# HGRN2 recurrence of a two-layer transformer: pair products of two neighbouring levels in one TensorE visit

## The chip, the cores and the metric

The kernel runs on one NeuronCore of a Trainium2 chip. The core has five engines that run side by side and meet at semaphores: TensorE (PE) for matrix products, VectorE (DVE) and ScalarE (ACT) for elementwise work, GpSimd (POOL), here for one kind of subtraction only, and SyncE (SP), which issues the transfers. The metric is the device time of one execution in microseconds; lower is better.

## The reference

Three blocks follow one another on 512 tokens of width 1024: a block with three mixers and a gated feed-forward part, a layer with an HGRN2 recurrence and a convolved feed-forward part, and a layer with latent attention. The change touches only the recurrence:

```
def _chunk_gated_recurrence(q, k, v, log_f):
    # S_t = diag(exp(log_f_t)) S_{t-1} + k_t v_t^T ; o_t = S_t^T q_t, chunkwise
    ...
        G = jnp.cumsum(gc, axis=2)
        ...
        diff = G[:, :, :, None, :] - G[:, :, None, :, :]
        decay = jnp.where(causal, jnp.exp(jnp.where(causal, diff, 0.0)), 0.0)
        scores = jnp.einsum("bhtd,bhsd,bhtsd->bhts", qc, kc, decay)
        o_intra = jnp.einsum("bhts,bhse->bhte", scores, vc)
```

There are 8 heads of width 128. For each head q, f (the forget gate), v (the values) and g (the output gate) are projections of the normed input.

## The kernel before

**Weights.** The products with weights are done in three parts, high half times high half, low times high and high times low, so that each 128 x 128 block of weights costs three matmuls of 512 columns (`products`, lines 228 to 230 of the profile). A unit is 8 such blocks. It comes in by a transfer, ACT makes its high half (`high`, L203) and POOL its low half in two instructions (L2900, L2901), in four slots that are used in turn. One projection tile is one unit: 24 matmuls, of which `pe_tile` can do a quarter (6 matmuls) at a time.

**Levels.** The causal scores of a head are taken in blocks of 128 tokens. Inside a block they are split by distance into seven levels of width 64, 32, 16, 8, 4, 2 and 1 (`LEVELS`, numbered 0 to 6), with the diagonal by itself ("own"). Each level passes through four steps:

- DVE takes the distances of the cumulated logarithms, two subtractions of 256 elements (`dve_distances`, L2038 and L2039).
- ACT takes their exponent (`act_decays`, L1939).
- DVE multiplies by key and query, 512 elements (`dve_factors`, L2048).
- PE makes the pair products in small tiles (`pe_level`, `pe_pairs`, L1777, 32 small matmuls for levels 2 to 6), and DVE copies the wanted half of them by a mask into the tile `diag` (`dve_keep_level`: a one-element copy at L2064 that only waits, and the copy at L2060).

Even levels go to one PSUM bank and odd ones to another, and `pe_level` waits for the copy of the level two before. The levels' operands take turns in four places, so `dve_distances` waits for the pair products of four levels before.

**Order on PE.** `pe_head(i)` writes the order by hand. It starts with `pe_attend(i - 1)` (L1742, L1745), which multiplies `diag` of the previous head by its values and so waits for the last copied level, 6, of that head. Then follow own and level 0, the tile f of head i + 1, the transposes of v (L422) and level 1. After that come the sum of squares of the previous head (`pe_finish`, L298), the products between blocks (`pe_across`, L1806), and the tiles q, g and v, in parts between the levels. `pe_across` waits for the previous head's `head_rstd` on ACT. In head 0 there are fewer tiles to place, so it holds matmuls whose results nobody reads (`pe_keep_busy`, L410). Head 7 has no next head; in place of tiles it takes steps of the output projection (`pe_project_step`, 9 matmuls each).

**Order on DVE.** `dve_head(i)` is written by hand too. From own on it runs: copy of own (L2171), `to_end` (L2175), copy of level 0, low squares (L2155), distances 3, factors 2, `dve_across` (L2141 to L2146), f, then copy of level 1, distances 4, factors 3, `dve_forget` (L2071 to L2077), `dve_normed` of the head before (L2121), q, copy 2, distances 5, factors 4, `dve_cum` (a scan, L2085), `dve_gated` (L2129), copy 3, distances 6, factors 5, `dve_low_out` (L2134), copy 4, factors 6, g, distances 0 of the next head, copy 5, distances 1 of the next head, copy 6. f, q, g and v leave PSUM at L402.

**Order on ACT.** `act_head` is not changed. It takes the decays in the order 2, 3, 4, 5, 6 and then 0 and 1 of the next head, and makes the highs of weight units in between. One is made after decays 6 and the copy of the products between blocks (L2005).

Of the kernel before, what the change touches and what calls it, by code (L numbers as in the profile page):

```python
# [27 lines left out]
LEVELS = (64, 32, 16, 8, 4, 2, 1)  # L28
# [206 lines left out]
def pe_tile(m, t, event, out, xh, xl, quarters=range(4)):  # L235

    base = take_unit(m, t)
    w = TILE
    for q in quarters:
        pairs = [(kb, xh[:, kb * w:(kb + 1) * w], xl[:, kb * w:(kb + 1) * w]) for kb in (2 * q, 2 * q + 1)]  # L240
        ins = products(m, t, out, base, pairs, start=q == 0, stop=q == 3)
        if q == 3:
            ins.then_inc(*m.U.mark(*event))
            t.unit += 1
# [162 lines left out]
def pe_keep_busy(m, t, bank, widths):  # L407

    for w in widths:
        t.op.matmul(bank[:, 0:w], m.col("ones", 0, P), m.col("levels", 0, w), start=True, stop=True)  # L410
# [1307 lines left out]
def level_bank(n):  # L1718
    return 0 if n % 2 else 3
# [49 lines left out]
def pe_pairs(m, t, left, right, event, bank, w):  # L1769


    n = max(w, 32)
    for c in range(0, S, P):
        for o in range(0, P, n if w < 32 else 2 * n):
            rows = slice(c + o, c + o + n)
            cols = rows if w < 32 else slice(c + o + n, c + o + 2 * n)
            ins = t.op.matmul(m.ab(bank)[o:o + n, cols], left[:, rows], right[:, cols], start=c == 0, stop=c == S - P,  # L1777
                              skip_group_check=True)
    ins.then_inc(*m.T.mark(*event))


def pe_level(m, t, i, n):
    x = Head(m, i).xs[n]
    t.wait_ge(*m.V.at("hgrn", "factors", i, n))
    if n > 1:
        t.wait_ge(*m.V.at("hgrn", "kept", i, n - 2))
    elif n:
        t.wait_ge(*m.V.at("hgrn", "kept_own", i))
    elif not i:
        t.wait_ge(*m.A.at("hgrn", "rstd"))  # L1790
    pe_pairs(m, t, x, x, ("hgrn", "pairs", i, n), level_bank(n), LEVELS[n])
# [18 lines left out]
def pe_head(m, t, i):  # L1810
    x = Head(m, i)
    last = i == KD - 1

    def f_tile():
        if i:
            t.wait_ge(*m.V.at("hgrn", "f", i))
        pe_tile(m, t, ("hgrn", "f", i + 1), f_bank(m, i + 1), m.nh, m.nl)

    def q_tile(quarters):
        t.wait_ge(*(m.A.at("hgrn", "o", i - 1) if i else m.V.at("hgrn", "q", 0)))  # L1820
        pe_tile(m, t, ("hgrn", "q", i + 1), m.gb(1), m.nh, m.nl, quarters)

    def g_tile(quarters):
        if i:
            t.wait_ge(*m.V.at("hgrn", "g", i - 1))
        pe_tile(m, t, ("hgrn", "g", i), m.gb(3), m.nh, m.nl, quarters)

    def v_tile(quarters):
        t.wait_ge(*m.A.at("hgrn", "vtok", i))
        pe_tile(m, t, ("hgrn", "v", i + 1), m.gb(2), m.nh, m.nl, quarters)  # L1830

    if i:
        pe_attend(m, t, i - 1)
    else:
        g_tile(range(4))
        f_tile()
    t.wait_ge(*m.V.at("hgrn", "key", i))
    t.wait_ge(*m.A.at("hgrn", "q", i))
    pe_pairs(m, t, x.key, x.qs, ("hgrn", "own", i), 0, 0)
    pe_level(m, t, i, 0)  # L1840
    if i and not last:
        f_tile()
    t.wait_ge(*m.V.at("hgrn", "v", i))
    pe_to_tokens(m, t, ("hgrn", "vtok", i), m.gb(2), x.vt, TB)
    if last:
        g_tile((0, 1))
    pe_level(m, t, i, 1)
    if i:
        pe_finish(m, t, i - 1)
    if last:  # L1850
        g_tile((2, 3))
    else:
        q_tile((0, 1))
    pe_level(m, t, i, 2)
    if last:
        pe_project_step(m, t, 0)
    else:
        q_tile((2, 3))
    pe_across(m, t, i)
    if last:  # L1860
        pe_project_step(m, t, 1)
    elif i:
        g_tile((0, 1))
    else:
        v_tile((0,))
    pe_level(m, t, i, 3)
    if last:
        pe_project_step(m, t, 2)
    elif i:
        g_tile((2, 3))  # L1870
    else:
        v_tile((1,))
    for n in range(4, len(LEVELS)):
        pe_level(m, t, i, n)
        if last:
            if n < 6:
                pe_project_step(m, t, n - 1)
        elif i:
            v_tile((0, 1) if n == 4 else (n - 3,))
        elif n < 6:  # L1880
            v_tile((n - 2,))
        if i == 0 and n in (4, 6):
            pe_keep_busy(m, t, m.gb(0), (512, 512) if n == 4 else (512, 512, 512))


def pe_project_step(m, t, kb):

    t.wait_ge(*m.V.at("hgrn", "low_out", kb))
    if kb == 0:
        t.wait_ge(*m.A.at("hgrn", "o", KD - 2))  # L1890
        t.wait_ge(*m.A.at("hgrn", "vtok", KD - 1))
    pe_wide(m, t, kb, [("ffn1", "projected", j) for j in range(WIDE)], m.bigr[:, 0:8 * TILE], m.bigr[:, 8 * TILE:16 * TILE])
# [138 lines left out]
def dve_distances(m, v, i, n):  # L2031
    x, w = Head(m, i), LEVELS[n]
    (g0, g1), (x0, x1) = halves(x.cum, w), halves(x.xs[n], w)
    mid = g0[:, :, w - 1:w].broadcast_to([P, S // (2 * w), w])
    before = level_before(i, n, 4)
    if before:
        v.wait_ge(*m.T.at("hgrn", "pairs", *before))
    v.op.tensor_tensor(x0, mid, g0, ALU.subtract)  # L2038
    v.op.tensor_tensor(x1, g1, mid, ALU.subtract).then_inc(*m.V.mark("hgrn", "distances", i, n))  # L2039


def dve_factors(m, v, i, n):
    x, w = Head(m, i), LEVELS[n]
    v.wait_ge(*m.A.at("hgrn", "decays", i, n))
    if n == 0:
        v.wait_ge(*m.A.at("hgrn", "q", i))
    xs = segments(x.xs[n], w)
    v.op.tensor_tensor(xs, xs, left_and_right(x.pair, w), ALU.mult).then_inc(*m.V.mark("hgrn", "factors", i, n))  # L2048


def dve_keep_level(m, v, i, n):

    w, pairs = LEVELS[n], P // (2 * LEVELS[n])
    mask = halves(m.col("levels", n * P, P), w)[1].bitcast(U32)
    mask = mask.broadcast_to([P, TB, w]) if pairs == 1 else mask.unsqueeze(1).broadcast_to([P, TB, pairs, w])
    part = lambda ap: blocks(ap).rearrange("p c (n a w) -> p c n a w", a=2, w=w)[:, :, :, 1, :]
    v.wait_ge(*m.T.at("hgrn", "pairs", i, n))
    v.wait_ge(*(m.V.at("hgrn", "kept", i, n - 1) if n else m.V.at("hgrn", "kept_own", i)))
    dve_wait_only(m, v)
    v.op.copy_predicated(part(Head(m).diag), mask, part(m.ab(level_bank(n)))).then_inc(*m.V.mark("hgrn", "kept", i, n))  # L2060
# [97 lines left out]
def dve_head(m, v, i):  # L2158
    x = Head(m, i)
    last = i == KD - 1  # L2160

    dve_factors(m, v, i, 0)
    dve_factors(m, v, i, 1)
    dve_distances(m, v, i, 2)
    if i:
        dve_v(m, v, i)
    v.wait_ge(*m.T.at("hgrn", "own", i))
    v.wait_ge(*(m.T.at("hgrn", "out", i - 1) if i else m.V.at("hgrn", "cleared")))
    dve_wait_only(m, v)
    mask = m.col("ident", 0, P).bitcast(U32).unsqueeze(1).broadcast_to([P, TB, P])  # L2170
    v.op.copy_predicated(blocks(x.diag), mask, blocks(m.ab(0))).then_inc(*m.V.mark("hgrn", "kept_own", i))  # L2171
    if i:
        v.wait_ge(*m.T.at("hgrn", "cross", i - 1))
    end = blocks(x.cum)[:, :, P - 1:P].broadcast_to([P, TB, P])
    v.op.tensor_tensor(blocks(x.kb), end, blocks(x.cum), ALU.subtract).then_inc(*m.V.mark("hgrn", "to_end", i))  # L2175
    dve_keep_level(m, v, i, 0)
    if i:
        dve_head_square_low(m, v, i - 1)
    dve_distances(m, v, i, 3)
    dve_factors(m, v, i, 2)  # L2180
    dve_across(m, v, i)
    if not last:
        dve_f(m, v, i + 1)
    dve_keep_level(m, v, i, 1)
    dve_distances(m, v, i, 4)
    dve_factors(m, v, i, 3)
    if not last:
        dve_forget(m, v, i + 1)
    if i:
        dve_normed(m, v, i - 1)  # L2190
    if not last:
        dve_q(m, v, i + 1)
    dve_keep_level(m, v, i, 2)
    dve_distances(m, v, i, 5)
    dve_factors(m, v, i, 4)
    if not last:
        dve_cum(m, v, i + 1)
    if i:
        dve_gated(m, v, i - 1)
    dve_keep_level(m, v, i, 3)  # L2200
    dve_distances(m, v, i, 6)
    dve_factors(m, v, i, 5)
    if i:
        dve_low_out(m, v, i - 1)
    dve_keep_level(m, v, i, 4)
    dve_factors(m, v, i, 6)
    dve_g(m, v, i)
    if not last:
        dve_distances(m, v, i + 1, 0)
    dve_keep_level(m, v, i, 5)  # L2210
    if not last:
        dve_distances(m, v, i + 1, 1)
    dve_keep_level(m, v, i, 6)


# [908 lines left out]
```

## Time and profile before

| | before |
|---|---|
| median of 3 runs | 2015.29 us (2014.92 to 2015.47) |
| the profiled execution | 2015.5 us, span 2013.7 us |
| granted TensorE clock | 1.000 of full speed over the span |
| PE busy | 1993.1 us, 99% of the span |
| DVE, ACT, POOL busy | 48%, 47%, 43% of the span |
| recurrence, heads 0 to 7 | about 820 to 1060 us of the span |
| DVE busy in 877 to 908 us (one head) | 28.42 of 31 us |
| DVE busy in 820 to 846 us (head 0) | 25.38 of 26 us |

An engine's busy share is an average over the span. The chain that ended last is 92% PE. Times in the rows below are microseconds from the span's start. A row of the timeline holds the start, the duration, the engine, the line and what is written from what, and in brackets how long the engine idled before it and what released it. A vector instruction's listed duration overlaps the next one's start by some 0.08 us, so for a run of them the distance from start to start is what counts.

### The profile page before, as it was taken

The page shows a single profiled execution, that of the slowest core. Times are in us where ns is not written, and L with a number is a line of the kernel's source. Part 1 is how long each engine was busy: PE and PEld are TensorE (multiplying, and loading weights), DVE is VectorE, ACT ScalarE, POOL GpSimd, SP SyncE. Part 2 cuts the span into 40 slices and gives each one's busy share as a digit, 9 for nine tenths or more (in the row PEclk, how much of TensorE's full clock was granted, in tenths as well). Part 3 has the DMA queues.
Part 4 walks back from the last instruction along what each step waited for, and adds up shares of the span by engine and source line. Part 5 has one row for each costly group of instructions (what it writes and reads, how often), then busy time and mean ns, then how long its engine had stood idle before and what let it go on. Part 6 is the DMA issues. An engine that isn't in the chain of part 4 may idle for free.

```text
span 2013.7 us, 26586 instructions
## 1 busy us (share of the span) xinstructions
PE 1993.1 (99%) x10917; PEld 1621.0 (80%) x10917; DVE 975.9 (48%) x1511; ACT 940.9 (47%) x1322; POOL 860.7 (43%) x670
## 2 busy tenths in 40 slices
PE   9999999999999999999999999999999999999999
PEld 7788888878888887677777888888877788888887
DVE  6644443254201315898984553255157645522551
ACT  6666663353223225666664543244267645432441
POOL 2344334526544543443334544444431255444443
PEclk9999999999999999999999999999999999999999
DMA  6122222223232221121212223222210222322231
GB/s 259 53 94 74 74 74 94 95 74 105 95 104 94 94 99 58 64 74 64 75 64 94 94 98 102 88 101 97 86 48 27 79 94 95 101 98 92 97 102 66
DMA packets 51817, 178.31 MB, mean 89 GB/s; under 512 B 5744, under 2 KB 8944, under 8 KB 51568
## 3 DMA queue, kind: packets, MB, share of 16 engines
q1 hardware_dynamic: 51696, 176.61, 26.0%
q8 instruction: 87, 1.43, 0.3%
q14 instruction: 34, 0.28, 0.0%
HBM read 174.49 MB, written 2.10 MB: 88 GB/s over the span
## 4 chain that ended last, share of the span: by engine, by line
PE 92%; DVE 5%; ACT 2%; issue 1%; DMA 0%; POOL 0%; SPq 0%; ACTq 0%; DVEq 0%; POOLq 0%
PE ps_gemm L228 24%; PE ps_gemm L230 24%; PE ps_gemm L229 24%; PE ps_attend L228 4%; PE ps_attend L230 4%; PE ps_attend L229 4%; PE ps_attend L912 1%; PE ps_attend L1777 1%; PE ps_attend L2620 1%; PE ps_attend L2687 1%; PE ps_attend L2622 0%; PE ps_attend L925 0%; PE ps_attend L2621 0%; PE ps_attend L285 0%; ACT weights_high L203 0%
## 5 line engine op out<-in xcount | busy, mean ns | idle before, releaser
L2900 POOL TENSOR_TENSOR weights_low<-weights_raw,weights_high 128x512 fp32r<-128x512 f32 (+1 forms) x331 | 433.0, 1308 | 1108.0 <-ACT weights_high L203 1107.8
L228 PE MATMUL ps_gemm<-normed_high,weights_high 128*128 128x512 f32 x1665 | 658.3, 395 | 3.9 <-DVE normed_low L1322 3.3
L230 PE MATMUL ps_gemm<-normed_low,weights_high 128*128 128x512 f32 x1665 | 646.9, 389 | 0.0
L229 PE MATMUL ps_gemm<-normed_high,weights_low 128*128 128x512 f32 x1665 | 646.4, 388 | 0.0
L203 ACT ACTIVATE weights_high<-weights_raw 128x1024 fp32r<-128x1024 f32 (+1 forms) x340 | 339.4, 1006 | 447.0 <-PE ps_attend L230 215.6
L2901 POOL TENSOR_TENSOR weights_low<-weights_raw,weights_high 128x512 fp32r<-128x512 f32 (+1 forms) x331 | 437.8, 1323 | 0.0
L228 PEld LDWEIGHTS ps_gemm<-normed_high,weights_high 128*128 128x128 f32 x1665 | 312.6, 188 | 74.3 <-DVE normed_low L1322 5.0
L230 PEld LDWEIGHTS ps_gemm<-normed_low,weights_high 128*128 128x128 f32 x1665 | 312.6, 188 | 65.0
L229 PEld LDWEIGHTS ps_gemm<-normed_high,weights_low 128*128 128x128 f32 x1665 | 312.8, 188 | 63.5 <-issue 1.9
L228 PE MATMUL ps_gemm<-operands_high_low,weights_high 128*128 128x512 f32 (+1 forms) x552 | 216.1, 392 | 0.8 <-ACT weights_high L203 0.3
L230 PE MATMUL ps_gemm<-operands_high_low,weights_high 128*128 128x512 f32 (+1 forms) x552 | 214.1, 388 | 0.0
L229 PE MATMUL ps_gemm<-operands_high_low,weights_low 128*128 128x512 f32 (+1 forms) x552 | 214.0, 388 | 0.0
L402 DVE TENSOR_TENSOR scratch<-ps_gemm,rstd 128x512 f32<-128x512 f32 x89 | 60.7, 687 | 215.3 <-PE ps_gemm L230 198.6
L402 DVE TENSOR_TENSOR squares<-ps_gemm,rstd 128x512 f32<-128x512 f32 x106 | 73.1, 689 | 160.8 <-PE ps_gemm L230 130.0
L1491 ACT ACTIVATE ps_attend<-squares,parameters 128x512 f32<-128x512 f32 x88 | 68.9, 783 | 170.1 <-DVE squares L402 170.1
L228 PE MATMUL ps_attend<-operands_high_low,weights_high 128*128 128x512 f32 (+1 forms) x336 | 127.5, 379 | 2.6 <-DVE operands_high_low L321 1.6
L230 PE MATMUL ps_attend<-operands_high_low,weights_high 128*128 128x512 f32 (+1 forms) x336 | 126.5, 376 | 0.0
L229 PE MATMUL ps_attend<-operands_high_low,weights_low 128*128 128x512 f32 (+1 forms) x336 | 126.5, 376 | 0.0
L228 PEld LDWEIGHTS ps_gemm<-operands_high_low,weights_high 128*128 128x128 f32 x552 | 103.7, 188 | 23.2 <-issue 1.1
L230 PEld LDWEIGHTS ps_gemm<-operands_high_low,weights_high 128*128 128x128 f32 x552 | 103.6, 188 | 21.2
L229 PEld LDWEIGHTS ps_gemm<-operands_high_low,weights_low 128*128 128x128 f32 x552 | 103.7, 188 | 20.9 <-issue 0.2
L1551 DVE SCALAR_TENSOR_TENSOR ps_attend<-squares,parameters,ps_attend 128x511 f32<-128x511 f32 x88 | 66.4, 755 | 76.1 <-ACT ps_attend L1491 76.1
(340 smaller groups left out, 2179.1 us busy)
## 6 DMA issues: line engine op xcount, KB each, us to landing
weights_raw<-weights_full SPq DMA_DIRECT2D x317, 512.0 KB, 3.2
weights_raw<-weights_short SPq DMA_DIRECT2D x24, 128.0 KB, 2.0
residual<-x_tiles SPq DMA_DIRECT2D x4, 512.0 KB, 7.5
out_tiles<-residual SPq DMA_DIRECT2D x8, 256.0 KB, 2.1
parameters<-params SPq DMA_DIRECT2D x1, 1559.5 KB, 10.4
scratch<-memory_tiles SPq DMA_DIRECT2D x2, 256.0 KB, 4.9
scratch<-memory_tiles SPq DMA_DIRECT2D x1, 512.0 KB, 5.8
scratch<-positions SPq DMA_DIRECT2D x1, 256.0 KB, 10.6
```

The source lines that it names most:

```text
L203: s.op.activation(m.wh[:, j * UNIT:j * UNIT + w], m.raw[:, j * UNIT:j * UNIT + w], ACT.Copy).then_inc(m.s_hi, 1)
L228: t.op.matmul(out, m.wh[:, c:c + P], xh, start=start and n == 0, stop=False, skip_group_check=True)
L229: t.op.matmul(out, m.wl[:, c:c + P], xh, start=False, stop=False, skip_group_check=True)
L230: ins = t.op.matmul(out, m.wh[:, c:c + P], xl, start=False, stop=stop and n == len(pairs) - 1, skip_group_check=True)
L402: return v.op.tensor_tensor(dst, ps, m.rstd[:, 0:dst.shape[1]], ALU.mult)
L912: ins = t.op.matmul(zb[:, o:o + S - j * P], neg_tri if j == kb else neg_ones, x[:, ZOFF[j]:ZOFF[j] + S - j * P], start=False, stop=False, ...
L1491: s.op.activation(y, m.sq_tile(half), ACT.Identity, bias=m.col(f"conv_b{n - 1}", c), scale=m.col(f"conv_w{n - 1}", 88 + c)).then_inc(*m.A. ...
L1551: v.op.scalar_tensor_tensor(out=y[:, 1:S], in0=u[:, 0:S - 1], scalar=w(1), in1=y[:, 1:S], op0=ALU.mult, op1=ALU.add).then_inc(*m.V.mark(st ...
L1777: ins = t.op.matmul(m.ab(bank)[o:o + n, cols], left[:, rows], right[:, cols], start=c == 0, stop=c == S - P, skip_group_check=True)
L2620: t.op.matmul(out, q_hi[:, qb * P:n], k_hi[:, 0:n], start=qb != 0 and k == 0, stop=False, skip_group_check=True)
L2900: g.op.tensor_tensor(m.wl[:, a], m.raw[:, a], m.wh[:, a].bitcast(F32), ALU.subtract)
L2901: g.op.tensor_tensor(m.wl[:, b], m.raw[:, b], m.wh[:, b].bitcast(F32), ALU.subtract).then_inc(m.s_lo, 1)
```

## The change

On PE, `pe_head` makes levels 1 and 2, 3 and 4, and 5 and 6 directly one after the other. The tiles that stood between the two levels of a pair move behind (or ahead of) the pair. In heads 1 to 6 the q tile is made in one piece. In head 0, three of the five matmuls of `pe_keep_busy` are left out and the other two stand at the end of the head. In head 7 the last projection step stands behind level 6 and so ahead of `pe_attend(7)`. On DVE, the copy of level 2 moves up to that of level 1, the copies of 3 and 4 stand together behind factors 5, and distances 1 of the next head moves ahead of the copy of level 5. No instruction of DVE is added or left out.

```
@@ pe_head
     if last:
         g_tile((0, 1))
+    elif not i:
+        q_tile((0, 1))
     pe_level(m, t, i, 1)
+    pe_level(m, t, i, 2)
     if i:
         pe_finish(m, t, i - 1)
     if last:
         g_tile((2, 3))
-    else:
-        q_tile((0, 1))
-    pe_level(m, t, i, 2)
-    if last:
         pe_project_step(m, t, 0)
+    elif i:
+        q_tile(range(4))
     else:
         q_tile((2, 3))
     pe_across(m, t, i)
@@
     elif i:
         g_tile((0, 1))
     else:
-        v_tile((0,))
+        v_tile((0, 1))
     pe_level(m, t, i, 3)
+    pe_level(m, t, i, 4)
     if last:
         pe_project_step(m, t, 2)
+        pe_project_step(m, t, 3)
     elif i:
         g_tile((2, 3))
+        v_tile((0, 1))
     else:
-        v_tile((1,))
-    for n in range(4, len(LEVELS)):
-        pe_level(m, t, i, n)
-        if last:
-            if n < 6:
-                pe_project_step(m, t, n - 1)
-        elif i:
-            v_tile((0, 1) if n == 4 else (n - 3,))
-        elif n < 6:
-            v_tile((n - 2,))
-        if i == 0 and n in (4, 6):
-            pe_keep_busy(m, t, m.gb(0), (512, 512) if n == 4 else (512, 512, 512))
+        v_tile((2, 3))
+    pe_level(m, t, i, 5)
+    pe_level(m, t, i, 6)
+    if last:
+        pe_project_step(m, t, 4)
+    elif i:
+        v_tile((2, 3))
+    else:
+        pe_keep_busy(m, t, m.gb(0), (512, 512))
@@ dve_head
     dve_keep_level(m, v, i, 1)
+    dve_keep_level(m, v, i, 2)
     dve_distances(m, v, i, 4)
     dve_factors(m, v, i, 3)
...
-    dve_keep_level(m, v, i, 2)
     dve_distances(m, v, i, 5)
     dve_factors(m, v, i, 4)
...
-    dve_keep_level(m, v, i, 3)
     dve_distances(m, v, i, 6)
     dve_factors(m, v, i, 5)
+    dve_keep_level(m, v, i, 3)
+    dve_keep_level(m, v, i, 4)
     if i:
         dve_low_out(m, v, i - 1)
-    dve_keep_level(m, v, i, 4)
     dve_factors(m, v, i, 6)
     dve_g(m, v, i)
     if not last:
         dve_distances(m, v, i + 1, 0)
+        dve_distances(m, v, i + 1, 1)
     dve_keep_level(m, v, i, 5)
-    if not last:
-        dve_distances(m, v, i + 1, 1)
     dve_keep_level(m, v, i, 6)
```

## Rows read from the trace of the kernel before

**Rows 1.** Timeline of PE around the visit for level 6 and the attend (head 2)

```profile
876.79 1.13 PE L1742 MATMUL ps_gemm<-scratch 128*128 128x128 f32 x8
...
903.80 0.39 PE L230 MATMUL ps_gemm<-normed_low,weights_high 128*128 128x512 f32 x1
904.12 0.46 PE L1777 MATMUL ps_attend<-parameters 128*32 128x32 f32 x32
904.50 0.50 PE L228 MATMUL ps_gemm<-normed_high,weights_high 128*128 128x512 f32 x1
904.84 0.39 PE L229 MATMUL ps_gemm<-normed_high,weights_low 128*128 128x512 f32 x1
...
908.00 0.35 PE L1742 MATMUL ps_gemm<-scratch 128*128 128x128 f32 x1
```

**Rows 2.** Timeline of DVE in the same head

```profile
889.71 0.55 DVE L2071 TENSOR_SCALAR scratch<-scratch,small 128x512 f32<-128x512 f32 x1 [0.46 <-ACT scratch L1951]
...
892.41 1.60 DVE L2121 SCALAR_TENSOR_TENSOR scratch<-scratch,parameters 128x512 f32<-128x512 f32 x1 [1.36 <-ACT scratch L292]
...
895.41 1.51 DVE L2039 TENSOR_TENSOR parameters<-scratch 128x256 f32<-128x256 f32 x1
...
899.31 0.15 DVE L2064 COPY small<-small 128x1 f32<-128x1 f32 x1
...
899.70 0.41 DVE L2038 TENSOR_TENSOR scratch<-scratch 128x256 f32<-128x256 f32 x1
...
901.96 0.84 DVE L2048 TENSOR_TENSOR scratch<-scratch 128x512 f32<-128x512 f32 x1
902.72 0.69 DVE L402 TENSOR_TENSOR scratch<-ps_gemm,rstd 128x512 f32<-128x512 f32 x1
...
904.34 1.50 DVE L2039 TENSOR_TENSOR squares<-scratch 128x256 f32<-128x256 f32 x1
905.77 0.14 DVE L2064 COPY small<-small 128x1 f32<-128x1 f32 x1
...
907.12 0.73 DVE L2060 COPY_PREDICATED scratch<-parameters,ps_attend 128x256 f32<-128x256 uint32 x1
...
910.90 0.15 DVE L2064 COPY small<-small 128x1 f32<-128x1 f32 x1 [0.66 <-PE ps_attend L1777]
```

**Rows 3.** Timeline of ACT in the same head, decays 6 and the high behind it

```profile
900.49 0.63 ACT L1939 ACTIVATE scratch<-scratch 128x512 f32<-128x512 f32 x1 [0.43 <-DVE scratch L2039]
...
901.71 1.05 ACT L203 ACTIVATE weights_high<-weights_raw 128x1024 fp32r<-128x1024 f32 x1
```

**Rows 4.** Timeline of POOL in the same head

```profile
895.17 1.48 POOL L2901 TENSOR_TENSOR weights_low<-weights_raw,weights_high 128x512 fp32r<-128x512 f32 x1
...
902.84 1.30 POOL L2900 TENSOR_TENSOR weights_low<-weights_raw,weights_high 128x512 fp32r<-128x512 f32 x1 [6.20 <-ACT weights_high L203]
```

**Rows 5.** Timeline of DVE at the end of head 0

```profile
838.81 0.68 DVE L2048 TENSOR_TENSOR squares<-squares,scratch 128x512 f32<-128x512 f32 x1
...
841.15 0.41 DVE L2038 TENSOR_TENSOR parameters<-scratch 128x256 f32<-128x256 f32 x1
...
844.71 0.71 DVE L2060 COPY_PREDICATED scratch<-parameters,ps_attend 128x256 f32<-128x256 uint32 x1
```

**Rows 6.** Timeline of ACT and POOL at the end of head 0

```profile
838.92 0.63 ACT L1939 ACTIVATE squares<-squares 128x512 f32<-128x512 f32 x1 [0.71 <-DVE squares L2039]
...
841.27 1.76 POOL L2900 TENSOR_TENSOR weights_low<-weights_raw,weights_high 128x512 fp32r<-128x512 f32 x1 [2.67 <-ACT weights_high L203]
```

**Rows 7.** Timeline of PE at the ends of heads 0 and 7

```profile
845.57 0.68 PE L1742 MATMUL ps_gemm<-scratch 128*128 128x128 f32 x4 [0.85 <-DVE scratch L2060]
...
1059.97 0.79 PE L1742 MATMUL ps_attend<-scratch 128*128 128x128 f32 x5 [1.01 <-DVE scratch L2060]
```

**Rows 8.** Timeline of POOL and DVE at the start of head 7

```profile
1033.74 1.27 POOL L2900 TENSOR_TENSOR weights_low<-weights_raw,weights_high 128x512 fp32r<-128x512 f32 x1 [3.27 <-ACT weights_high L203]
...
1033.79 1.50 DVE L2038 TENSOR_TENSOR parameters<-scratch 128x256 f32<-128x256 f32 x1
```

## Prediction

> **What bounds the kernel now.** I began with the page: PE is busy 99% of the span and the chain that ended last is 92% PE, so time should follow PE. The list of PE's waits in the recurrence agrees on first reading: the attend, which reads the finished `diag`, waits for DVE's last masked copy by more than a fraction only in head 0, 0.85 us, and once more in head 7, 1.01 us [rows 7]. For heads 1 to 6 it lists nothing. There one would count what PE saves and be done.
>
> The third view says otherwise. I laid the end of the last copy beside the start of the attend. In head 0 the copy ends at 844.71 + 0.71 = 845.42 [rows 5] and the attend, which did wait, starts 0.15 later [rows 7]. In head 2 the copy ends at 907.12 + 0.73 = 907.85 [rows 2] and the attend starts at 908.00 [rows 1], again 0.15 later. The other middle heads show the same distance. So the attend is released by DVE in every head; PE arrives at almost the same moment, and the profile lists no idle time that short. Two loops of equal length run side by side. One is PE's own work, 31.2 us for a head, as from the attend at 876.79 to that at 908.00 [rows 1]. The other goes from the copy of level 6 through attend and own (908.00 to about 910.75, where DVE's wait of 0.66 us for own ends [rows 2]) and then through DVE and ACT to the next copy of level 6. Within that second part DVE waits twice, both times for ACT: 0.46 us for the sigmoid and 1.36 us for `head_rstd` [rows 2]. It waits for PE nowhere. Shortening PE's work alone therefore moves nothing; the second loop has to shorten.
>
> **Part 1: fewer visits on PE.** A big matmul starts every 0.23 us, as 904.84 would have followed 903.80 by two such steps, 0.46. With the visit between them it takes 1.04, so a visit costs 0.58, of which 904.12 to 904.50, 0.38, is the visit itself [rows 1]. Entering and leaving cost 0.20. Each merged pair saves it once: three in a head, 0.6 us, all on PE's loop. In heads 1 to 6 its loop becomes 30.6 us, and that gain is hidden as long as the DVE loop stays longer.
>
> **Part 2: the copy of level 2 moves up.** It costs 899.31 to 899.70, 0.39 us with its waiting copy [rows 2]. It now falls ahead of the 0.46 us wait for the sigmoid and fills it. Pairs 2 are ready, since PE makes them right behind level 1. The place that it leaves lies between q and distances 5. There the second subtraction takes 1.51 us in place of 0.41 [rows 2]; it ends at 896.92, when POOL's subtraction of 895.17 + 1.48 = 896.65 has let go [rows 4]. POOL starts there from ACT's chain behind f, which does not move. So distances 5 begins 0.39 earlier and ends at the same time: gain 0. Had POOL not been there it would be 0.39 a head; this is the upper bound.
>
> What the row shows is one engine standing still until the other's instruction ends. The Trainium skill says so too, in "SBUF — State Buffer", section "Who interferes with whom": a DVE instruction with two SBUF inputs contends with a GpSimd instruction that reads SBUF, and the later one blocks fully. Here the trace agrees, 1.51 us against 0.41 [rows 2].
>
> **Part 3: copies 3 and 4 behind factors 5.** Distances 6 starts at 899.31 in place of 899.70, so decays 6 and the high behind it on ACT (900.49 and 901.71 [rows 3]) are 0.39 earlier, and POOL is ready for its third unit at 902.84 - 0.39 = 902.45 [rows 4]. Up to the end of factors 6 DVE does the same work as before, so factors 6 still runs from 901.96 to 902.72 and reads two SBUF tiles [rows 2]. POOL gets in behind it at about 902.69, 0.15 earlier than before. Distances 0 of the next head waits for both of POOL's instructions (1.50 us for the second subtraction [rows 2]) and so ends 0.15 earlier. Bounds: 0 if POOL keeps its time, 0.39 if it gets in first. Nearest is the row of factors 6 itself, so I take 0.15.
>
> **Part 4: distances 1 before copy 5.** From 905.77 to 907.12 DVE does the waiting copy, copy 5, distances 1 and the next waiting copy, 1.35 us [rows 2]. The new order has the same terms: 0. What is moved up for ACT (decays 1) isn't late in the middle heads.
>
> **Waits the change adds.** Level 4 now follows level 3 at once, 2.9 us earlier on PE, and needs factors 4, which starts at 895.41 + 1.51 - 0.07 = 896.85 and ends some 0.7 us later [rows 2]. PE would be there at about 897.6, so it may wait about 0.1 us, with g and v queued behind; it has 0.45 to spare. Level 6 needs factors 6 and is asked for at about 904: free by then.
>
> **Heads 1 to 6:** 6 x 0.15 = 0.9 us gained. PE's attend then waits about 0.6 - 0.15 = 0.45 us in each.
>
> **Head 0.** DVE has no slack, so its order decides. Factors 5 starts at 838.81 and distances 0 of the next head at 841.15, 2.34 us later [rows 5]. POOL asks at 841.27 [rows 6], just behind, so the first two subtractions got through. Now copy 3 stands behind factors 5 too. All ahead of it is 0.39 earlier, POOL's turn with it (840.88), but DVE comes to distances 0 only at 841.15, so POOL is first by 0.27. From POOL's start to the end of the last copy it is then as in head 2: 905.77 - 902.84 = 2.93, 1.35 and 0.73 [rows 2, 4], 5.01 in all. Copy 6 ends at 845.89, the attend starts at 846.04 in place of 845.57: 0.47 us lost. Had DVE been first, about 1.0 would be gained. The three filler matmuls left out cost nothing, as PE waited at their end.
>
> **Head 7.** Here PE goes ahead of DVE. The 1.01 us wait before `pe_attend(7)` [rows 7] goes, since a projection step of 9 matmuls (over 2 us) now stands between level 6 and it. Three visits fewer give 0.6. Against this, copy 2 stands ahead of distances 4, which ACT needs for decays 4 and then `head_rstd`, for which `pe_across` waits; that takes back 0.3 to 0.4. I count 1.25. A lock decides more than that: at the head's start POOL took the port at 1033.74, 0.05 before DVE's subtraction at 1033.79, which then took 1.50 [rows 8]. POOL's start follows decays 1, now some 0.75 us earlier, and falls again next to the start of a DVE instruction. If DVE gets through, about 1 us more is gained, if not, up to 1.3 is lost. I leave it at 0.
>
> **Sum.** The profiled execution took 2015.5, 0.2 above the median. 2015.5 - 0.9 + 0.47 - 1.25 = 2013.8; against the median 2013.6.
>
> **Rivals.**
> - PE is the bound after all, or the DVE loop shortens as much as PE's. Then 0.6 in each of six heads, 3.6, and 1.25 to 2.2 in head 7: 2015.3 - 4.9 to 5.8 = 2009.5 to 2010.4. For it: the chain runs through PE alone in these heads. Against it: the distance of 0.15 us. Chance 0.24.
> - DVE's order gains more, since POOL misses a subtraction somewhere (0.4 a head or head 0's 1.0): 2011 to 2012. Chance 0.15, half of it over the bound.
> - Slower, by TensorE's clock. It is 1.000 throughout the span of before. At the end of head 0 three filler matmuls go, and by the working above PE would stand idle for close to 3 us before the attend, against 0.85 now [rows 7]. If the clock falls from 2.4 to 1.2 GHz there, attend and own (2.75 us [rows 1, 2]) take twice as long, and as they lie in the loop nothing hides it; a low clock through the f tile costs 5.5 more. From 2013.6 that is 2016.4 to 2022. It decides if the low clock outlasts own by 3 us. "TensorE: Matmul & The Clock Gate", section "HAM oscillation — how this bites in real kernels", of the Trainium skill warns of such idle gaps; no row here shows a fall. Chance 0.08, 0.05 of it over the bound.
> - The forecast, 2012 to 2015.5: chance 0.53.
>
> **How the numbers follow.** Below 0.2% (4 us, about what a measurement here can tell from no change) lies the forecast with all but the PE-bound rival. Faster 0.24 + 0.07 = 0.31; slower 0.05; same 0.64. The range goes from the PE-bound case to the forecast with 1.3 lost in head 7 and a little of the clock: 2009.5 to 2016.3.
>
> **What would show it.** In the profile after: a PE wait of 0.3 to 0.5 us for L2060 before each L1742 of heads 1 to 6, and a head of about 31.05 us from own to own. No such wait and 30.6 us would prove the first rival. In head 0 the attend at 846.0 with both subtractions of distances 0 blocked; in head 7 no wait before its last attend. A granted clock under 1.00 near 846 would prove the third. The forecast is wrong if POOL's starts don't follow ACT's highs as reckoned.

## The result and the profile after

| | before | after |
|---|---|---|
| median | 2015.74 us (16 runs, 2014.92 to 2016.76) | 2019.54 us (16 runs, 2017.82 to 2022.31) |
| profiled execution | 2015.5, span 2013.7 | 2017.85, span 2016.1 |
| mean granted clock of the runs | 1.000, rarely 0.999 | 0.996 to 0.999 |

The ratio after to before is 1.002, 95% interval 1.0014 to 1.0026. The change makes the kernel slower, by 3.8 us between the medians. Two facts have to be told apart: the lowest run is already 2.9 us slower than the lowest of before, and the runs lie 4.5 us apart, where those of before lie 1.8 apart.

The waits of PE in 810 to 1070 us of the kernel after (total, times, longest):

```profile
PE ps_gemm L1742 <- DVE scratch L2061: 7.4, 7, 1.7
PE ps_gemm L422 <- DVE scratch L402: 2.1, 1, 2.1
PE ps_attend L1777 <- DVE scratch L2061: 1.6, 1, 1.6
...
```

The first row is the prediction's main point: the attend now waits visibly in each of heads 0 to 6, for DVE's last masked copy (one line further down in this kernel). In head 2 it is this row of PE's timeline:

```profile
909.82 1.13 PE L1742 MATMUL ps_gemm<-scratch 128*128 128x128 f32 x8 [0.94 <-DVE scratch L2061]
```

The wait is 0.94 us, not 0.45, and from this attend back to the one before it is 31.52 us, where it was 31.2 [rows 1]. So PE did save its 0.6 us, and DVE's loop became longer by 0.3. DVE in head 2, after (start, duration):

```profile
889.09 0.43 DVE L2061 COPY_PREDICATED scratch<-parameters,ps_attend 128x256 f32<-128x256 uint32 x1
889.62 0.15 DVE L2065 COPY small<-small 128x1 f32<-128x1 f32 x1
...
902.17 0.43 DVE L2061 COPY_PREDICATED scratch<-parameters,ps_attend 128x256 f32<-128x256 uint32 x1
902.70 0.15 DVE L2065 COPY small<-small 128x1 f32<-128x1 f32 x1
...
903.70 0.83 DVE L2049 TENSOR_TENSOR scratch<-scratch 128x512 f32<-128x512 f32 x1
904.46 0.68 DVE L402 TENSOR_TENSOR scratch<-ps_gemm,rstd 128x512 f32<-128x512 f32 x1
...
907.33 0.41 DVE L2039 TENSOR_TENSOR squares<-scratch 128x256 f32<-128x256 f32 x1
...
908.06 0.72 DVE L2061 COPY_PREDICATED scratch<-parameters,ps_attend 128x256 f32<-128x256 uint32 x1
908.89 0.15 DVE L2065 COPY small<-small 128x1 f32<-128x1 f32 x1
908.96 0.71 DVE L2061 COPY_PREDICATED scratch<-parameters,ps_attend 128x256 f32<-128x256 uint32 x1
```

Each masked copy waits for the copy of the level before (`kept`), as both write `diag`. Before the change something else always ran between two copies, and the wait cost nothing. Now the second copy of a pair starts only when the first has ended and signalled: 889.62 is 0.53 after 889.09, where the instruction behind a copy otherwise starts 0.33 after it (902.77 to the next at 903.10, as 899.31 to 899.70 with its waiting copy made 0.39 [rows 2]). For level 6 it is 908.89 - 908.06 = 0.83 in place of 0.52 (before, the instruction behind the copy of 907.12 started at 907.64). From the start of distances 1 (907.33) to the last copy (908.96) is 1.63, where the same instructions took 1.35 from 905.77 to 907.12 [rows 2].

POOL in the same head, after:

```profile
903.99 1.71 POOL L2900 TENSOR_TENSOR weights_low<-weights_raw,weights_high 128x512 fp32r<-128x512 f32 x1 [5.81 <-ACT weights_high L203]
905.66 1.46 POOL L2901 TENSOR_TENSOR weights_low<-weights_raw,weights_high 128x512 fp32r<-128x512 f32 x1
```

Here the mechanism of the prediction is seen at work. POOL is ready at 903.99, during factors 6, and must let it pass: 1.71 us in place of 1.30 [rows 4], so it gets in at about 904.4. But factors 6 is itself 0.2 us late, by the pair of copies 3 and 4, and the 0.15 us that POOL should have come earlier are gone.

The second fact is the clock. The stretches of head 0 after, in slices of 1 us (third number from the end: granted clock):

```profile
842.00:843.00 1.00, 1.00 (x2) 0.45 (x3) 1.00 (x2) 0.00 (x0) 1.00 (x2) 0.68 0.00 0
843.00:844.00 1.00, 1.00 (x2) 0.34 (x1) 1.00 (x1) 0.00 (x0) 1.00 (x1) 0.50 0.00 0
844.00:845.00 1.00, 1.00 (x2) 0.00 (x0) 1.00 (x4) 0.58 (x1) 0.11 (x1) 0.50 0.00 0
845.00:846.00 1.00, 0.12 (x1) 0.00 (x0) 0.90 (x5) 0.68 (x2) 0.00 (x0) 0.61 0.84 221
```

Before it falls, PE has waited twice, for level 5 and for level 6:

```profile
840.19 0.46 PE L1777 MATMUL ps_attend<-squares 128*32 128x32 f32 x32 [1.62 <-DVE scratch L2061]
841.44 0.46 PE L1777 MATMUL ps_attend<-squares 128*32 128x32 f32 x32 [0.78 <-DVE squares L2049]
```

At about 842.3 the clock falls from 2.4 to 1.2 GHz (0.50), and it is back at 845.7. In this execution the low stretch falls on the two fillers and on idle time, so it costs nothing. That is luck; other executions show it later, on products that count. The runs' mean clock goes with their times: six runs at 0.999 took 2017.82 to 2019.36, nine at 0.998 took 2018.95 to 2021.24, and the one at 0.996 took 2022.31.

The third place is the start of head 7. POOL, DVE and PE there, after:

```profile
1036.21 1.56 POOL L2900 TENSOR_TENSOR weights_low<-weights_raw,weights_high 128x512 fp32r<-128x512 f32 x1 [2.64 <-ACT weights_high L203]
1037.72 1.72 POOL L2901 TENSOR_TENSOR weights_low<-weights_raw,weights_high 128x512 fp32r<-128x512 f32 x1
```

```profile
1035.92 2.39 DVE L2049 TENSOR_TENSOR squares<-squares,scratch 128x512 f32<-128x512 f32 x2
1038.24 1.49 DVE L2039 TENSOR_TENSOR parameters<-scratch 128x256 f32<-128x256 f32 x1
1039.65 1.49 DVE L2040 TENSOR_TENSOR parameters<-scratch 128x256 f32<-128x256 f32 x1
1041.06 0.68 DVE L402 TENSOR_TENSOR scratch<-ps_gemm,rstd 128x512 f32<-128x512 f32 x1
```

```profile
1041.79 0.66 PE L422 MATMUL ps_gemm<-parameters,scratch 128*128 128x128 f32 x4 [2.10 <-DVE scratch L402]
```

POOL starts 0.29 us behind DVE's factors 0 (1035.92), where it started 1.18 behind it before (1033.74 against 1032.56). So it comes in between factors 0 and factors 1 (together 2.39 us), and three of DVE's instructions are blocked in turn in place of two, of which [rows 8] has the first. The second of them, and PE's wait for v, before the change:

```profile
1035.22 1.49 DVE L2039 TENSOR_TENSOR parameters<-scratch 128x256 f32<-128x256 f32 x1
```

```profile
1037.37 0.66 PE L422 MATMUL ps_gemm<-parameters,scratch 128*128 128x128 f32 x4 [1.03 <-DVE scratch L402]
```

PE now waits 2.10 us for v in place of 1.03.

### The profile page after: what moved, and what is told of

It is laid out like the page before. It is cut to its first block, busy times and chain, and to the rows that moved or that the text cites. A ratio compares the mean times of both kernels' runs of the same rounds, so it can differ in the third digit from the quotient of the medians.

```text
span 2016.1 us, 26587 instructions
## 1 busy us (share of the span) xinstructions
PE 1986.6 (99%) x10911; PEld 1621.0 (80%) x10911; DVE 981.3 (49%) x1511; ACT 941.8 (47%) x1322; POOL 864.2 (43%) x670
## 4 chain that ended last, share of the span: by engine, by line
PE 85%; DVE 11%; ACT 3%; issue 1%; DMA 0%; POOL 0%; SPq 0%; DVEq 0%; ACTq 0%; POOLq 0%
PE ps_gemm L228 22%; PE ps_gemm L229 22%; PE ps_gemm L230 22%; PE ps_attend L228 4%; PE ps_attend L229 4%; PE ps_attend L230 4%; PE ps_attend L912 1%; DVE scratch L2061 1%; DVE scratch L402 1%; PE ps_attend L2687 1%; ACT weights_high L203 1%; DVE squares L2040 1%; PE ps_attend L2620 1%; DVE squares L2049 1%; DVE squares L2039 1%
```

## The experiments

Where "head" stands below, it is the distance between two attends in the profiled execution; "last" is from the attend of head 6 to that of head 7 and "first" the attend of head 0 from the first pair product. The medians are of 10 or 11 runs, that of after of 16. The medians of before taken beside them are 2015.79 (for pe_only, part56, spread and fillers), 2015.86 (ballast, mid_only, old_head0 and after_look) and 2015.94 (before56, fillers56 and head6_end).

| kernel | first | heads 1 to 6 | last | median (lowest to highest) | runs at clock 1.000 |
|---|---|---|---|---|---|
| before | 25.33 | 31.22 | 27.06 | 2015.8 | most |
| after | 26.10 | 31.52, one 31.85 | 26.19 | 2019.54 (2017.82 to 2022.31) | 0 of 16 |
| after_look | 26.07 | 31.52, one 32.42 | 27.78 | 2019.90 (one run) | 0 of 1 |
| pe_only | 25.35 | 31.22 | 25.77 | 2015.78 (2014.34 to 2016.73) | 0 of 11 |
| ballast | 26.09 | 31.52, three longer | 27.86 | 2020.10 (2017.85 to 2022.03) | 0 of 10 |
| part56 | 25.80 | 31.24, two longer | 26.14 | 2015.98 (2014.88 to 2019.17) | 0 of 11 |
| spread | 25.75 | 31.05, two longer | 25.75 | 2015.12 (2013.70 to 2016.92) | 0 of 11 |
| before56 | 24.33 | 31.50, one 31.40 | 28.13 | 2018.38 (2016.98 to 2020.09) | 6 of 11 |
| fillers | 26.08 | 31.53, one 31.85 | 26.19 | 2018.90 (2017.52 to 2021.20) | 4 of 11 |
| fillers56 | 25.78 | 31.25, one 31.59 | 25.86 | 2015.65 (2015.04 to 2015.98) | 11 of 11 |
| mid_only | 25.33 | 31.52, one 32.38 | 29.70 | 2019.59 (2018.64 to 2021.19) | 5 of 11 |
| head6_end | 25.34 | 31.52, others 31.25 to 31.85 | 26.45 | 2017.32 (2016.92 to 2017.91) | 8 of 11 |
| old_head0 | 25.31 | 31.04 | 26.20 | 2013.41 (2012.98 to 2014.75) | 11 of 11 |

### Is the attend released by DVE? (pe_only, ballast)

pe_only takes PE's new order with DVE's old one.

```diff
 # pe_head as after; dve_head as before:
-    dve_keep_level(m, v, i, 1); dve_keep_level(m, v, i, 2)
+    dve_keep_level(m, v, i, 1)
+    ...   # 2, 3, 4, 5 and 6 each at its old place
```

> TensorE's new order alone, DVE's order as before the change. Theory of two loops (the attend is released by DVE, PE's saving of 0.6 us a head is hidden): a head stays at 31.2 us, PE shows a wait of about 0.6 us before each attend; only head 7 gains, 1.0 of its end wait and 0.3 to 0.6 of visits: 2014.0 to 2014.5, plus up to 2 if the clock falls in head 0. Rival (PE is the bound before the change): 30.6 us a head, no wait, 2010.5.

PE in head 2 of pe_only:

```profile
908.30 0.91 PE L1742 MATMUL ps_gemm<-scratch 128*128 128x128 f32 x6 [0.66 <-DVE scratch L2061]
```

Heads of 31.22 us to the hundredth, as before the change, and a wait of 0.66 that was not there. PE's saving is real and hidden. Only the last stretch gains, 1.3 us. Its lowest run, 2014.34, which is the profiled one, has that gain; the median, 2015.78, is no better than before, and 2014.0 to 2014.5 was expected if the clock held. No run has a clock of 1.000. In the trace the clock is low at 841 to 845 us, on the fillers, where it costs nothing; that it falls later in the other runs and eats the gain is likely, but no trace of this kernel shows it.

ballast puts work of 0.47 us into the wait instead.

```diff
     elif i:
         v_tile((2, 3))
+        pe_keep_busy(m, t, m.gb(0), (256,))
```

> The changed kernel with one matmul of 256 columns, whose result nobody reads, behind v in heads 1 to 6, 0.47 us each on TensorE. Two loops: it fits into the wait of 0.94 us before the attend, heads stay at 31.5 us, time as the changed kernel, 2019.5. Rival (TensorE sets the time in heads 1 to 6): +0.47 x 6 = 2.8 us.

PE in head 2 of ballast:

```profile
910.00 0.59 PE L410 MATMUL ps_gemm<-parameters 128*128 128x256 f32 x2
911.09 1.13 PE L1742 MATMUL ps_gemm<-scratch 128*128 128x128 f32 x8 [0.49 <-DVE scratch L2062]
```

The filler takes 0.4 to 0.5 us out of the wait of 0.94 and the head stays at 31.52. The median is 0.6 above the changed kernel's, where 2.8 were at stake.

### What do neighbouring copies cost? (part56, spread, before56)

```diff
 # part56, on the kernel after
         dve_distances(m, v, i + 1, 0)
-        dve_distances(m, v, i + 1, 1)
     dve_keep_level(m, v, i, 5)
+    if not last:
+        dve_distances(m, v, i + 1, 1)
     dve_keep_level(m, v, i, 6)
```

> The changed kernel with distances 1 of the next head back between the copies of levels 5 and 6. Theory D (a masked copy directly behind another waits for the first to finish writing, 0.2 us for levels 2 and 4, 0.3 for level 6, and this lengthens the loop DVE - attend): one head becomes 31.52 - 0.3 = 31.2 us, head 0 also 0.3 shorter, and at the start of head 7 POOL is late again, so the wait for v there is 1.0 in place of 2.1 us: in all 3 us less than the changed kernel, lock and clock apart. Rival L (the loop is longer because POOL's subtraction moved, the copies cost nothing): heads stay at 31.5 us. The clock may still fall in head 0.

Heads of 31.24 as reckoned, the wait for v at 1.04, the median 3.6 us under the changed kernel's. Taking this one pair of copies apart is worth 0.28 us a head.

spread takes the other two pairs apart as well, on top of part56.

```diff
     dve_keep_level(m, v, i, 1)
-    dve_keep_level(m, v, i, 2)
     dve_distances(m, v, i, 4)
+    dve_keep_level(m, v, i, 2)
...
     dve_distances(m, v, i, 6)
+    dve_keep_level(m, v, i, 3)
     dve_factors(m, v, i, 5)
-    dve_keep_level(m, v, i, 3)
     dve_keep_level(m, v, i, 4)
```

> The changed kernel, TensorE's order kept, with no two masked copies next to each other on DVE (copy 2 behind distances 4, copy 3 between distances 6 and factors 5, distances 1 between copies 5 and 6). Theory D: besides part56's gain factors 6 ends 0.2 us earlier and POOL gets in at the time reckoned in the prediction: one head 31.05 to 31.1 us, attend waits 0.45 us, median about 4 us under the changed kernel, clock apart. Rival L: as the changed kernel, 31.5 us a head.

31.05 us a head and a wait of 0.46 to 0.50: this is the time and the wait that the prediction gave for heads 1 to 6 of the changed kernel. Factors 6 starts 25.19 us behind the attend (997.17 - 971.98), as before the change (901.96 - 876.79 = 25.17), where it is 25.40 in the changed kernel (903.70 - 878.30), and POOL gets in 0.2 earlier with it. The reckoning of the lock between POOL and DVE was right, then, and what it lacked was the cost of the pairs. The edit doesn't tell the pair 1 and 2 from the pair 3 and 4; the rows put the 0.2 us on 3 and 4, since behind 1 and 2 DVE waits for `head_rstd` on ACT in any case, 1.31 us in the changed kernel.

before56 makes the one edit in the kernel before, where PE's order is the old one.

```diff
 # before56, on the kernel before
         dve_distances(m, v, i + 1, 0)
-    dve_keep_level(m, v, i, 5)
-    if not last:
         dve_distances(m, v, i + 1, 1)
+    dve_keep_level(m, v, i, 5)
     dve_keep_level(m, v, i, 6)
```

> The kernel before with one edit: distances 1 of the next head ahead of the copy of level 5, so that copies 5 and 6 stand directly behind each other on DVE. Theory D: +0.3 us in each of heads 1 to 6 although no instruction is added (31.5 in place of 31.2), and head 7's wait for v becomes 2.1 us in place of 1.0, since ACT's high and POOL come earlier to the shared port there: 2015.8 + 1.8 + 1.1 = 2018.7, plus up to 1.6 if the clock falls behind the wait of 2.1. Rival: the order of the same instructions costs nothing, 2015.8.

DVE in head 2 of before56, and PE's wait for v over the recurrence:

```profile
905.50 0.73 DVE L2060 COPY_PREDICATED scratch<-parameters,ps_attend 128x256 f32<-128x256 uint32 x1
906.34 0.15 DVE L2064 COPY small<-small 128x1 f32<-128x1 f32 x1
906.41 0.72 DVE L2060 COPY_PREDICATED scratch<-parameters,ps_attend 128x256 f32<-128x256 uint32 x1
```

```profile
PE ps_gemm L422 <- DVE scratch L402: 2.1, 1, 2.1
```

Two neighbouring instructions changed places, none was added, and the kernel is 2.4 us slower (ratio 1.0012, interval 1.0003 to 1.0021). The copies start 0.91 apart. Both costs appear without any change on PE: 0.28 in each head and 1.07 in head 7. One thing was not expected: head 0 is 1.0 us shorter. There the two subtractions of distances 1 directly follow those of distances 0 and also run before POOL gets in, 0.41 us each in place of 0.92 and 1.49. The profiled execution, 2016.98, is the lowest of the eleven; the other 1.4 us up to the median have no trace.

### Where does the clock fall? (after_look, fillers, mid_only, head6_end, fillers56)

after_look is the changed kernel itself, once more.

> The changed kernel once more, for a second trace: where its clock is low. Theory C: around 842 to 852 us in head 0 and the start of head 1, at another place than in the first trace, and the span longer by what of it falls on weight matmuls. Rival: somewhere in heads 1 to 7.

Its clock is low from 841.1 to 844.5 and, in head 7, here:

```profile
1041.00:1042.00 1.00, 0.00 (x0) 0.00 (x0) 1.00 (x4) 0.69 (x2) 1.00 (x2) 1.00 0.94 328
1042.00:1043.00 1.00, 0.97 (x6) 0.88 (x7) 1.00 (x3) 0.04 (x1) 0.51 (x1) 0.75 0.32 127
1043.00:1044.00 1.00, 1.00 (x4) 0.81 (x3) 1.00 (x4) 0.63 (x1) 0.00 (x0) 0.50 0.44 98
1044.00:1045.00 1.00, 1.00 (x4) 0.81 (x3) 1.00 (x4) 0.05 (x1) 0.00 (x0) 0.50 0.91 373
1045.00:1046.00 1.00, 1.00 (x4) 0.72 (x4) 1.00 (x2) 1.00 (x2) 0.00 (x0) 0.54 0.14 53
```

So theory C was half of it: there is a second place, right behind the wait of 2.10 us for v. The first slice shows PE idle at full clock. At half clock a big matmul starts every 0.43 us (1043.39, 1043.82, 1044.24), where it is 0.23 at full clock. The last stretch is 27.78 us against 26.19 in the first trace, 1.6 more. This execution took 2019.90. Its attend of head 0 comes 26.07 us after the first pair product, just as in the first trace, since the low clock fell on fillers again. When it falls behind them it costs, as in part56, where PE waited 1.61 and 0.77 us before levels 5 and 6 too, but the clock stayed at 1.00 until the longer wait before the attend:

```profile
846.12 1.71 PE L1742 MATMUL ps_gemm<-scratch 128*128 128x128 f32 x8 [2.71 <-DVE scratch L2061]
```

```profile
846.00:847.00 1.00, 0.88 (x6) 0.91 (x7) 1.00 (x2) 0.00 (x0) 0.00 (x0) 0.75 0.30 119
847.00:848.00 1.00, 1.00 (x5) 0.96 (x5) 1.00 (x4) 0.00 (x0) 0.00 (x0) 0.50 0.00 0
848.00:849.00 1.00, 1.00 (x3) 0.43 (x2) 0.36 (x1) 0.00 (x0) 0.00 (x0) 0.50 0.00 0
849.00:850.00 1.00, 1.00 (x5) 0.82 (x3) 0.00 (x0) 0.00 (x0) 0.00 (x0) 0.55 0.00 0
```

The attend and own of head 1 run at half speed, and that head takes 32.91 us in place of 31.24, 1.7 more (32.49 against 31.05 in spread, 33.04 against 31.52 in ballast, where PE had been idle 2.90 and 2.99 us before the attend). So with the new order on PE in head 0 and without the three fillers the clock fell in all six traces, in three of them at 841 to 842 (after, after_look, pe_only) and in three at 846 to 847.

fillers puts the five filler matmuls of head 0 back.

```diff
     else:
+        pe_keep_busy(m, t, m.gb(0), (512, 512))
         v_tile((2, 3))
     pe_level(m, t, i, 5)
...
     else:
-        pe_keep_busy(m, t, m.gb(0), (512, 512))
+        pe_keep_busy(m, t, m.gb(0), (512, 512, 512))
```

> The changed kernel with the five filler matmuls of head 0 back (two ahead of v's second half, three after level 6). Theory C (the three missing fillers let TensorE's clock fall in head 0, to 0.50 in 843 to 845 us of the profiled run, and in most runs for longer than the idle time there): mean clock 1.000, all runs within about 2 us of each other, median near the lowest runs of the changed kernel, 2017.8 (-1.7 against its median 2019.54). Rival (the spread and the extra time have another source, the vector engine's order): median stays 2019 to 2020, with the same spread of 4.5 us. Attends of heads 1 to 6 wait 0.9 us as in the changed kernel under both.

The profiled execution has a clock of 1.000 and 2017.75 us, but the median only falls to 2018.90 and 7 of 11 runs still lie below 1.000. The forecast of 2017.8 missed. The second place, which this edit doesn't touch, is the likely reason: its trace has the wait of 2.10 us for v, at full clock.

mid_only leaves heads 0 and 7 as before and changes heads 1 to 6.

```diff
+def pe_head(m, t, i):
+    (pe_head_new if 0 < i < KD - 1 else pe_head_old)(m, t, i)   # dve_head alike
```

> The change in heads 1 to 6 alone; heads 0 and 7 as before. Copies theory: heads of 31.5 us (+0.3 each, one of them 31.85), the wait for v at the start of head 7 is 2.1 us since DVE's order at the end of head 6 is the new one, end wait of head 7 back at 1.0: 2015.8 + 2.1 + 1.1 = 2019. If the clock falls only in head 0, it is 1.000 here and the runs lie close together; if the waits of 0.94 us in the middle heads lower it, 0.999 and a spread of 3 us or more.

2019.59 against the 2019 expected. Head 0 stands at 25.33 as before. The waits of 0.94 in the middle heads didn't lower the clock in its trace; the clock is low from 1042.3 to 1045.7 alone, behind the wait of 2.10 us. Here the last stretch is 29.7 long.

head6_end is mid_only with distances 1 of head 7 back between copies 5 and 6 of head 6.

```diff
         dve_distances(m, v, i + 1, 0)
-        dve_distances(m, v, i + 1, 1)
+    if i < KD - 2:
+        dve_distances(m, v, i + 1, 1)
     dve_keep_level(m, v, i, 5)
+    if i == KD - 2:
+        dve_distances(m, v, i + 1, 1)
     dve_keep_level(m, v, i, 6)
```

> mid_only with the end of head 6 on DVE as before the change (distances 1 of head 7 between copies 5 and 6). If the wait of 2.1 us for v at the start of head 7 comes from there and lowers the clock behind it: wait 1.0 us, last stretch 27.1 in place of 28.1 to 29.7, clock 1.000, 2017.3 with runs within 2 us. Rival (wait and clock come from the longer waits in heads 1 to 6): wait 2.1 or clock 0.999, 2019.6 as mid_only.

2017.32, where 2017.3 was expected, the runs within 1.0 us, 8 of 11 at 1.000 and the others at 0.999, where 1.000 was expected. In its trace there is no wait for v at all, so the last stretch is 0.6 shorter than reckoned. One pair of instructions moved in one head is worth 2.3 us.

fillers56 mends both places.

> The changed kernel with the fillers of head 0 back and distances 1 between copies 5 and 6: both places at which the traces show a fallen clock mended. Theory C: 1.000 in every run, heads 31.24, 2017.6 (lowest runs of fillers) - 0.3 x 6 - 1.1 = 2014.6, runs within 2 us. Rival (one of the two is not the cause): 0.999 in most runs and a median of 2016, as part56.

11 of 11 runs at 1.000, within 0.94 us of each other. With neither place mended it was 0 of 16, with head 0 alone (fillers) 4 of 11, with the copies 5 and 6 alone (part56) 0 of 11: both places together are the cause of the spread. The time missed the forecast by 1.05: I had counted 1.1 us for the end of the wait for v, but PE then waits 1.53 us for factors 1 in the same place, and the last stretch gains 0.33 alone (25.86 against 26.19).

### A version that is faster than both (old_head0)

Head 0 stays as before on both engines; heads 1 to 7 have PE's new order and spread's order on DVE.

```diff
+def pe_head(m, t, i):
+    (pe_head_new if i else pe_head_old)(m, t, i)
+def dve_head(m, v, i):
+    (dve_head_new if i else dve_head_old)(m, v, i)   # dve_head_new as in spread
```

> Head 0 on both engines as before the change; heads 1 to 7 with the new order on TensorE and the order of spread on DVE (no two masked copies next to each other). Theory C (what is lost in head 0 is the longer idle time of TensorE and the clock that falls in it): granted clock 1.000, first attend at about 845.6 us, heads 31.05 us, last 25.75: 2015.8 - 6 x 0.17 - 1.3 = 2013.5 and runs within 2 us of each other. Rival (the clock falls because of the waits of 0.5 us before each attend, not because of head 0): clock 0.999 and 2015, spread of 3 us, as in spread.

PE in head 2 of old_head0:

```profile
908.15 1.02 PE L1742 MATMUL ps_gemm<-scratch 128*128 128x128 f32 x7 [0.44 <-DVE scratch L2141]
```

2013.41 us, ratio to before 0.9988 (0.9979 to 0.9997), heads of 31.04, every run at clock 1.000. The last stretch is 26.20, not the 25.75 expected, with a wait of 1.04 for v that spread's trace doesn't have. Against spread only the order in head 0 differs, and with it go 1.7 us of the median and the low clock.

## Why the prediction was wrong

**The bound.** Right. The distance of 0.15 us between the last copy's end and the attend did mean that DVE releases it in every head: pe_only shows that 0.6 us less of PE's work moves nothing, and ballast that 0.5 us more moves nothing in the changed kernel.

**Part 1.** Right: pe_only's wait of 0.66 is the saving of three visits.

**Part 2.** Right in its result, gain 0: behind the pair of copies the wait for the sigmoid is gone and distances 5 ends where it did. But the wait of 0.46 us had kept DVE in step with POOL. Without it the last instruction of `dve_forget` starts 0.06 us later relative to POOL (0.01 ahead of it in head 2, where it was 0.07), and in head 3 the two meet. In the trace of after, POOL then DVE:

```profile
923.75 1.57 POOL L2900 TENSOR_TENSOR weights_low<-weights_raw,weights_high 128x512 fp32r<-128x512 f32 x1 [3.81 <-ACT weights_high L203]
```

```profile
923.73 0.43 DVE L2077 TENSOR_SCALAR scratch<-scratch 128x512 f32<-128x512 f32 x1
924.08 1.52 DVE L2078 TENSOR_SCALAR scratch<-scratch 128x512 f32<-128x512 f32 x1
```

The last of its three instructions is blocked, and that head takes 31.85. In after_look the last two are, and it takes 32.42. It is 0.3 or 0.9 us, and neither was in the sum.

**Parts 3 and 4.** Here the prediction failed. "Up to the end of factors 6 DVE does the same work as before" and "The new order has the same terms: 0" are true of instructions and false of time. The semaphore between one masked copy and the next was in the code and cost nothing as long as something stood between them. Measured: 0.28 us a head for copies 5 and 6 (31.52 to 31.24 in part56, 31.22 to 31.50 in before56), and 0.19 for the other pairs (31.24 to 31.05 in spread), which is what kept POOL from coming the reckoned 0.15 earlier. So a head came to +0.3 in place of -0.15, 2.7 us over six heads. This step alone brings the forecast to the upper bound of its range, 2013.6 + 2.7 = 2016.3; the same pair in head 0 (0.3), head 3's lock (0.33) and the smaller gain in head 7 (0.38) carry it over. The execution of fillers at a clock of 1.000, 2017.75, shows what these orders take without a low clock.

**Head 0.** Sign and mechanism right: both subtractions are blocked. Measured 26.10 - 25.33 = 0.77 in place of 0.47; the 0.3 more is the pair of copies 5 and 6, as part56 shows with 25.80.

**Head 7.** The end wait went and the visits were saved. The lock was left at 0 and fell to the bad side: PE's wait for v is 1.07 longer. All six traces with copies 5 and 6 together at the end of head 6 have this wait (after, after_look, ballast, fillers, mid_only, before56) and none of the others, so it was no throw of a coin: it follows from decays 1, and ACT's high and POOL behind it, coming some 0.9 us earlier against DVE. In before56 it cost the stretch 1.07; in the changed kernel less, since without it PE waits elsewhere (26.19 against 26.14 in part56 and 25.86 in fillers56). The stretch gave 0.87 in place of 1.25.

**The clock.** The third rival, with 0.08, happened as well, though only in half in the place that was named. Its share of the median is about 1.8 us (2019.54 against 2017.75), less than that of the copies. That the measured time lies inside this rival's 2016.4 to 2022 is therefore luck. In head 0 the clock falls and that costs nothing or 1.4 to 1.7 us. Where it costs (part56, spread, ballast) it fell behind 2.7 to 3.0 us of idle time before the attend, the place and the length that the prediction had; where it costs nothing (after, after_look, pe_only) it fell earlier, behind the waits for levels 5 and 6. In the changed kernel the larger part seems to lie in head 7, behind the longer wait for v, 1.6 us when it falls: with the fillers back the median still lies 1.15 above 2017.75. I had not looked for idle time there.

**The sum.** In the profiled executions: head 0 +0.77, heads 1 to 6 +1.8 and 0.33 for head 3's lock, head 7 -0.87, together 2.0 of the 2.35 between them; the first pair product was 0.45 later to begin with, from stages that the change doesn't touch. In after_look with head 3 at +0.9 more and the clock low in head 7 it is 0.74 + 1.75 + 0.9 + 0.72 = 4.1, where 4.0 were measured to the median of before. The median is most likely of that second kind.

## What to carry to other kernels

If an engine looks fully busy, compare the end of what it takes from another engine with its own start, head by head; a constant small distance points to a second loop of the same length, and then shortening the first is worth nothing. A step moved on an engine is paid for at its new neighbours: look for semaphores between instructions of the same engine, since two that wait for each other's result want something between them. After a change of order, look again at every wait of PE of more than a microsecond, also in stages that gained, and at the lowest and highest run, as a clock that falls in some executions shows there first.

## What the runs showed of the hardware

- The clock can fall behind a single wait of 2.10 us, and whether it does differs from one execution to the next. Behind this wait for v in head 7 it fell to 0.50 in three traces (after_look, ballast, mid_only) and stayed at 1.00 in three (after, fillers, before56). Each fall lasted about 3.4 us and cost 1.4 to 1.7 us where it met products that count.
- On DVE the one-element copy that waits for the masked copy directly before it starts 0.10 us after that one's listed end (889.62 against 889.52), where an instruction that doesn't wait for it starts 0.1 to 0.2 us before that end (903.10 against 903.20).
- Where DVE and POOL block each other, an order that turns on 0.02 us decides 0.6 us. In after, POOL at 923.75 lets DVE's instruction of 923.73 pass; in after_look POOL starts at 923.45 and DVE's of 923.47 takes 1.56 us:

```profile
923.45 1.29 POOL L2900 TENSOR_TENSOR weights_low<-weights_raw,weights_high 128x512 fp32r<-128x512 f32 x1 [3.80 <-ACT weights_high L203]
```

```profile
923.47 1.56 DVE L2077 TENSOR_SCALAR scratch<-scratch 128x512 f32<-128x512 f32 x1
```

What stays open is how often each of these outcomes occurs, since only the profiled execution of a kernel has a trace. The falls in the traces don't account for every run either: two of 3.4 us make a mean clock of 0.998, while a run of the changed kernel at 0.996 would need some 16 us at half clock (estimate: 0.004 x 2020 / 0.5), and two runs of spread at 0.997 some 12, where its trace has one fall. The semaphore between the masked copies was not taken away by itself, as both write one tile; its cost rests on the distances in the rows and on the three kernels that move the copies apart or together.
